# Up projections by pairs of tiles, in three orders of the float32r and bfloat16 products

## What is computed

```python
D_MODEL, SEQ, DEPTH, D_FF = 1024, 512, 4, 2816

def _conv_ffn(h, w_up, conv_w, conv_b, w_down):
    u = _causal_dwconv(h @ w_up, conv_w, conv_b)
    return (jax.nn.silu(u[..., D_FF:]) * u[..., :D_FF]) @ w_down

for i in range(DEPTH):
    ...
    x = x + mix.astype(x.dtype)
    x = x + _conv_ffn(_rmsnorm(x, ffn_norm[i]), ffn_w_up[i], ffn_conv_w[i], ffn_conv_b[i],
                      ffn_w_down[i]).astype(x.dtype)
```

## Time and profile before

| | |
|---|---|
| median of 3 runs | 1731.17 us (1730.94 to 1731.2) |
| span of the profiled execution, first to last instruction | 1728.1 us |
| median less span (the execution's own whole time is not listed apart) | 3.1 us |
| TensorE busy | 1704.1 us, 99% |
| VectorE, ScalarE, GpSimd busy | 1148.4, 1098.1, 1230.8 us |
| up projection of layer 0, first to last product | 141.2 to 299.4 us |
| of layer 1 | 666.1 to 824.2 us |
| of layer 2 | 1033.7 to 1191.8 us |
| of layer 3 | 1486.8 to 1645.2 us |

### The profile page before, as it was taken

The page is one execution under the profiler, slowest core; times in us unless marked ns, Lnnn a source line. Parts: engine busy times, 40 slices in busy tenths (PEclk is TensorE's granted clock), DMA queues, the critical chain, the costliest instruction groups (busy, mean ns, idle before and its releaser), DMA issues.

```text
span 1728.1 us, 27117 instructions
## 1 busy us (share of the span) xinstructions
PE 1704.1 (99%) x9708; PEld 1031.6 (60%) x9708; DVE 1148.4 (66%) x1965; ACT 1098.1 (64%) x1566; POOL 1230.8 (71%) x1776
## 2 busy tenths in 40 slices
PE   7999999999999999999999999999999999999999
PEld 4556666655555556666665666666656665566665
DVE  6986777228888865777328858775247886677720
ACT  7887666446877756666445776665555665866632
POOL 7867777877556648777877657778766553777785
PEclk9999999999999999999999999999999999999999
DMA  7334444546233325544554124445433332444453
GB/s 273 113 98 134 147 147 142 157 151 177 74 98 100 96 86 169 150 147 148 151 152 132 38 74 140 147 148 153 150 122 102 96 99 75 134 149 147 148 157 119
DMA packets 65614, 226.53 MB, mean 131 GB/s; under 512 B 8149, under 2 KB 9045, under 8 KB 65109
## 3 DMA queue, kind: packets, MB, share of 16 engines
q1 hardware_dynamic: 64236, 221.89, 41.0%
q10 hardware_dynamic: 1245, 2.92, 0.6%
HBM read 222.48 MB, written 2.10 MB: 130 GB/s over the span
## 4 chain that ended last, share of the span: by engine, by line
PE 83%; ACT 7%; DVE 6%; issue 3%; POOL 1%; DMA 0%; SPq 0%; DVEq 0%; ACTq 0%; POOLq 0%
PE psum L310 26%; PE psum L320 25%; PE psum L352 13%; PE psum L356 12%; DVE psum L1655 1%; ACT w_big L251 1%; PE psum L2329 1%; PE psum L1884 1%; PE psum L2365 1%; ACT psum L1499 1%; ACT L1534 1%; PE psum L1929 1%; DVE arena L1700 1%; ACT psum L1534 1%; PE psum L2346 0%
## 5 line engine op out<-in xcount | busy, mean ns | idle before, releaser
L281 POOL TENSOR_TENSOR w_rest<-w_panel,w_big 128x256 bf16<-128x256 f32 x1660 | 1168.4, 741 | 419.9 <-ACT w_big L251 419.0
L310 PE MATMUL psum<-x_big,w_big 128*128 128x512 f32 x2248 | 653.0, 423 | 7.3 <-ACT x_big L402 6.5
L320 PE MATMUL psum<-x_rest,w_rest 128*128 128x512 bf16 x2248 | 555.9, 382 | 1.9 <-DVE x_rest L505 1.9
L251 ACT ACTIVATE w_big<-w_panel 128x1024 fp32r<-128x1024 f32 (+1 forms) x414 | 417.0, 1032 | 171.1 <-PE psum L356 95.4
L310 PEld LDWEIGHTS psum<-x_big,w_big 128*128 128x128 f32 x2248 | 415.7, 189 | 127.2 <-issue 18.2
L320 PEld LDWEIGHTS psum<-x_rest,w_rest 128*128 128x128 bf16 x2248 | 188.2, 98 | 281.5 <-issue 101.8
L738 DVE SCALAR_TENSOR_TENSOR psum<-ffn_raw,params,psum 128x512 f32<-128x512 f32 x352 | 264.4, 751 | 7.2 <-ACT psum L692 1.0
L730 DVE TENSOR_TENSOR ffn_raw<-psum,rstd 128x512 f32<-128x512 f32 x176 | 121.2, 691 | 129.0 <-PE psum L320 119.9
L692 ACT ACTIVATE psum<-ffn_raw,params 128x512 f32<-128x512 f32 x176 | 137.4, 782 | 101.2 <-DVE ffn_raw L730 101.0
L352 PE MATMUL psum<-g_big,w_big 128*128 128x512 f32 x704 | 199.6, 423 | 0.0
L572 DVE SCALAR_TENSOR_TENSOR x_resid<-psum,x_resid 128x512 f32<-128x512 f32 x64 | 43.8, 688 | 224.2 <-PE psum L356 216.3
(11 more groups left out here) (281 smaller groups left out, 1654.8 us busy)
## 6 DMA issues: line engine op xcount, KB each, us to landing
w_panel<-in_up SPq DMA_DIRECT2D x176, 512.0 KB, 3.5
w_panel<-in_dn SPq DMA_DIRECT2D x64, 448.0 KB, 3.2
w_panel<-in_ssd_in SPq DMA_DIRECT2D x41, 512.0 KB, 3.5
w_panel<-in_dn SPq DMA_DIRECT2D x32, 512.0 KB, 3.5
w_panel<-in_hgrn_in SPq DMA_DIRECT2D x32, 512.0 KB, 3.5
w_panel<-in_lru_in SPq DMA_DIRECT2D x18, 512.0 KB, 3.6
w_panel<-in_ssd_out SPq DMA_DIRECT2D x16, 512.0 KB, 3.5
w_panel<-in_swa_in SPq DMA_DIRECT2D x12, 512.0 KB, 3.5
```

The lines of the kernel that those rows point to most:

```text
L251: act.activation(k.w1[:, slot, 0:words], k.w[:, slot, 0:words], ACT.Copy, scale=(SHIFT - 1) / SHIFT).then_inc(k.s("panel_big"), 1)
L281: rest = pool.tensor_tensor(k.w2[:, slot, a], k.w[:, slot, a], k.w1[:, slot, a].bitcast(F32), ALU.subtract)
L310: pe.matmul(out, k.w1[:, slot, q * m:(q + 1) * m], k.x1[:, q, :], start=q == 0, stop=False)
L320: mm = pe.matmul(out, k.w2[:, slot, q * m:(q + 1) * m], k.x2[:, q, :], start=False, stop=q == DT - 1)
```

## The change

Tiles 0 and 1 of each up projection and the norm's products stay as they are. From tile 2 on the tiles are taken by pairs (2j, 2j+1), and each layer has its own order of the 32 products of a pair:

- layer 0 (`up_pair`): 8 float32r of the first tile, 8 of the second, 8 bfloat16 of the first, 8 of the second;
- layer 1 (`up_mixed`): the 16 float32r products with the two tiles taking turns, then, after a wait for both remainders, the 16 bfloat16 products likewise;
- layer 2 (`up_singles`): as before, tile by tile;
- layer 3 (`up_turns`): 8 float32r of the first tile; then, product by product, one float32r of the second tile and one bfloat16 of the first, eight times; then 8 bfloat16 of the second.

The number of products, waits and signals is the same; no other engine's program is touched.

```diff
+def up_singles(pe, k, job, first):
+
+    for i in (first, first + 1):
+        in_begin(pe, k, job, i)
+        in_tile(pe, k, job, i)
+
+
+def up_pair(pe, k, job, first):
+
+    for i in (first, first + 1):
+        in_begin(pe, k, job, i)
+        in_big(pe, k, job, i)
+    for i in (first, first + 1):
+        pe.wait_ge(k.s("panel_split"), k.split(job, i))
+        in_rest(pe, k, job, i)
+
+
+def up_mixed(pe, k, job, first):
+
+    for i in (first, first + 1):
+        in_begin(pe, k, job, i)
+    for q in range(DT):
+        for i in (first, first + 1):
+            in_big(pe, k, job, i, q, q + 1)
+    for i in (first, first + 1):
+        pe.wait_ge(k.s("panel_split"), k.split(job, i))
+    for q in range(DT):
+        for i in (first, first + 1):
+            in_rest(pe, k, job, i, q, q + 1)
+
+
+def up_turns(pe, k, job, first):
+
+    for i in (first, first + 1):
+        in_begin(pe, k, job, i)
+        if i == first:
+            in_big(pe, k, job, i)
+    pe.wait_ge(k.s("panel_split"), k.split(job, first))
+    for q in range(DT):
+        in_big(pe, k, job, first + 1, q, q + 1)
+        in_rest(pe, k, job, first, q, q + 1)
+    pe.wait_ge(k.s("panel_split"), k.split(job, first + 1))
+    in_rest(pe, k, job, first + 1)
+
+
 def ffn_tensor(pe, k, l):
 
     job = f"up{l}"
-    for i in range(2 * FF_T):
+    for i in range(2):
         in_begin(pe, k, job, i)
         in_big(pe, k, job, i, fresh=None if i else 2 * l + 1)
         pe.wait_ge(k.s("panel_split"), k.split(job, i))
         in_rest(pe, k, job, i, fresh=None if i else 2 * l + 1)
-        if i == 1:
-            norm_in_parts(pe, k, l)
+    norm_in_parts(pe, k, l)
+    for i in range(2, 2 * FF_T, 2):
+        (up_pair, up_mixed, up_singles, up_turns)[l](pe, k, job, i)
```

## The result

The changed kernel took 1734.18 us (median of 9 runs, 1733.67 to 1735.71), the kernel before beside it 1730.55 us (9 runs): a ratio of 1.0023, with a 95% interval of 1.0016 to 1.0031, or 3.6 us more. The forecast was 3.7 us more, from a median of 1731.17.

The account below looks back on a forecast made before the run. TensorE, busy 1704.1 of 1728.1 us, was taken as the bound, except in the changed layer 1. Layers 0 to 3 gave -0.4 + 1.9 + 0 + 2.2 = +3.7: 1734.9 us from 1731.17; own range 1733.5 to 1736.3, wider range 1732.0 to 1738.0.

Parts of the forecast that it names:

- the two effects named for it: Behind the own range: type switches at 10.5 ns give +3.0 us in sum; a chain link off by 0.1 moves 1.0.
- Layer 0: Up projection by `up_pair`: one round trip between types saved in each of 21 pairs, -0.4 us, with no wait.
- one cost for all round trips: TensorE's changes between float32r and bfloat16: 17.8 ns a round trip in the sums, 10.5 ns kept for the range.
- Layer 1: Up projection by `up_mixed`: chain over the other engines becomes the bound, 14.51 against 14.32 us per two pairs, +1.9 us.
- The excess of 0.19: Layer 1's chain over two pairs exceeds the former time by 0.19 us, in ten cycles.
- Layer 3: Up projection by `up_turns`: eight round trips a pair in place of two, +2.2 us, with no wait.
- Chain hidden: Layer 1: links overlap by 0.2 us more, TensorE stays the bound; +1.4 in sum, 1732.6 us; 15%.
- Changes of type are free: Layers 0 and 3: changes between types cost nothing, so both layers give nothing; 1733.1 us; 8%.
- Longer chain: Layer 1: chain 0.4 us longer over two pairs, the layer +5.9 us; 1738.9 us; 12%.
- Two banks cost 10 ns: Layers 1 and 3: products alternating between two banks cost 10 ns each, +6.3 and another 3.4 us; 1742.7 us; 5%.
- Float32r gains behind a bfloat16 product: Layer 3: single turns hide the float32r weight load, 2.2 us gained; with the chain hidden 1728.1 us; 4%.
- The clock: TensorE's granted clock should stay 1.00; at half, layer 1 alone takes 150 us more, 1881 us; 1%.

## Why the prediction was right, and where a size was off

**Sum and sign.** The time, the sum of the four layers (+3.57 against +3.7) and the place of each part came as forecast. Two terms were off in opposite directions, 0.4 too little saved in layer 0 and 0.6 too little lost in layer 1, and the third, 0.3 too much in layer 3, made up the rest. That the sum is within 0.1 is partly luck. (The forecast's own range, 1733.5 to 1736.3, is narrower below and wider above than the two effects named for it give: +3.0 less 1.0 is 1733.2, +3.7 and 1.0 is 1735.9.)

**Layer 0, mis-sized: 0.04 us for the round trip saved, not 0.018.** The step that failed is the formula behind it, which took one cost for all round trips from blocks of 1 and of 8 and 7 in other stages. A trip between single products costs 0.017 to 0.018, as taken, but one between blocks of 2 to 8 costs 0.026 to 0.040. Comparing single with longer blocks therefore understates the latter. The starts show where the 0.04 lies. In the pair from 213.37 the 16 float32r products take 217.21 - 213.37 - 0.19 = 3.65, against 2 x 1.84 = 3.68 tile by tile, and the 16 bfloat16 products 220.49 - 217.21 + 0.19 = 3.47, against 2 x 1.74 = 3.48. So most of it is a faster distance of float32r products late in a block: the seven steps from 213.78 on are 0.230 each (215.39 - 213.78 = 1.61), the next seven 0.227 (216.98 - 215.39 = 1.59).

```profile
213.78 0.39 PE L310 MATMUL psum<-x_big,w_big 128*128 128x512 f32 x1
...
215.39 0.39 PE L310 MATMUL psum<-x_big,w_big 128*128 128x512 f32 x1
...
216.98 0.39 PE L310 MATMUL psum<-x_big,w_big 128*128 128x512 f32 x1
```

The first float32r products behind a bfloat16 block are the slower ones; why, no run here shows.

**Layer 1, right in mechanism and place: +2.49 for +1.9.** The third pair was the first to wait, ten pairs waited, every second one, and each link read from the earlier trace rows came within 0.03. That the pairs between wait too, if only by 0.05, was not forecast. The cycle was 14.58 for 14.51. The difference lies at GpSimd's end: the remainder ended at 702.63 + 4.92 = 707.55, and the weight load of the first product it fed began at 707.66, 0.11 later (0.11 or 0.12 in all 19 pairs from the third on); the product stands 0.03 behind its load (714.87 and 714.84). Together that is 0.14, where the earlier trace rows gave 0.06 to the product itself.

```profile
702.63 4.92 POOL L281 TENSOR_TENSOR w_rest<-w_panel,w_big 128x256 bf16<-128x256 f32 x7
...
707.66 1.42 PEld L320 LDWEIGHTS psum<-x_rest,w_rest 128*128 128x128 bf16 x8 [0.54 <-POOL w_rest L281]
```

The excess of 0.19 over a sum of 14 us was rightly called thin, but it decided as read. Three runs show the cause: with the panels' terms ahead of the gating's followers it is gone, with the first tile released early it is gone, with the evictions moved it grows as the chain says.

**Layer 3: +1.90 for +2.2.** Seven further trips of 0.018 over a pair with one, against one further trip of 0.040 before: 0.129 - 0.040 = 0.089 us a pair, 21 x 0.089 = 1.9. The forecast had 6 x 0.0178 = 0.107.

**The rivals.** *Chain hidden*: fell, the waits are there. *Changes of type are free*, which the Trainium skill's rule of weight loads pulled ahead (TensorE: Matmul & The Clock Gate, Part 2) would give: fell, each round trip costs 0.017 to 0.040, and the load behind a change to bfloat16 is late even where nothing is waited for. *Longer chain*: a sixth of its 0.4 came true. *Two banks cost 10 ns*: fell, turns of both types took 157.33. *Float32r gains behind a bfloat16 product*: fell, the single turns of layer 3 are 0.460 apart and not below 0.4475. *The clock*: granted 1.00 in every run; cycling through two banks with short waits did not bring the loss that the Trainium skill (TensorE: Matmul & The Clock Gate, A second HAM failure mode) tells of in another kernel.

## What to carry to other kernels

Where TensorE is the bound, a regrouping of its products is worth little of itself (here 0.04 us for a round trip between the types saved, 0.2% in all), and its danger is in the release: two tiles that end together are handled one after the other, and everything queued behind the second comes later. Follow that through every in-order queue to what TensorE wants next, and compare the sum with the right number of periods: here two pairs, since the ring of four slots hands a panel's slot on to the pair after next. An edit that moves the visible late step can make it worse if the next queue waits for what it was moved past; moving the step that TensorE waits for (here ScalarE's terms of the next panels) is the cure.

## What the hardware showed that was not expected

- The distance of float32r products of 512 columns depends on what they read: 0.229 us ((1682.75 - 1677.52 - 0.19)/22) from `x_big` and 0.234 from `g_big`, in one stage and with the same weights' slots. Bfloat16 products are 0.216 ((4.92 - 0.38)/21 in the rows at 1224.31) or 0.217 apart with either.
- Within a block from `x_big` the first seven steps behind a bfloat16 block are 0.230 and the following 0.227.
- A change of type costs 0.017 us a round trip between single products, up to 0.040 between blocks of 8; longer blocks gained 0.03 a trip with `x_big` and next to nothing with `g_big`.
